# A projection chunk's matmul order: high weights on the front tokens first, then on the rear ones

## The reference

```python
x = x + 0.5 * swiglu(rmsnorm(x, p['ffn1_norm'][i]), p['ffn1_w_in'][i], p['ffn1_w_out'][i])
h = rmsnorm(x, p['mix_norm'][i])
...
x = x + y
x = x + cross_attend(rmsnorm(x, p['xattn_norm'][i]), mem_k[i], mem_v[i], p['xattn_w_q'][i], p['xattn_w_o'][i])
x = x + 0.5 * swiglu(rmsnorm(x, p['ffn2_norm'][i]), p['ffn2_w_in'][i], p['ffn2_w_out'][i])
```

```python
def swiglu(x, w_in, w_out):
    gate, up = jnp.split(x @ w_in, 2, axis=-1)
    return (jax.nn.silu(gate) * up) @ w_out
```

## Time and profile before

| | |
|---|---|
| runs | 2361.16, 2360.91, 2357.80 us; median 2360.91 |
| profiled execution, first to last instruction | 2357.9 us |
| PE busy | 2332.7 us (99%), 21043 matmuls |
| PEld busy | 2270.3 us (96%) |
| DVE busy | 1295.9 us (55%) |
| ACT busy | 869.0 us (37%) |
| POOL busy | 609.4 us (26%) |
| bytes moved | 289.19 MB, 123 GB/s over the span |
| the eight output halves begin at | 141, 344, 877, 1060, 1274, 1476, 2103, 2286 us |

### The profile page before, as it was taken

One profiled execution on the slowest core, in us unless ns is written; L12 is line 12 of the kernel. 1 busy time (PEld: TensorE's weight loads), 2 busy tenths in 40 slices (PEclk: granted clock), 3 DMA queues, 4 the chain that ended last, 5 costly groups with the idle time before them and its releaser, 6 DMA issues.

```text
span 2357.9 us, 50146 instructions
## 1 busy us (share of the span) xinstructions
PE 2332.7 (99%) x21043; PEld 2270.3 (96%) x21043; DVE 1295.9 (55%) x1906; ACT 869.0 (37%) x1399; POOL 609.4 (26%) x591
## 2 busy tenths in 40 slices
PE   8999999999999999999999999999999999999999
PEld 8999999889979999999999999999999979999999
DVE  6653643964576443445543344577777666443443
ACT  4422333453233321322433233267775233321323
POOL 4779967331103000004111010432122102000003
PEclk9999999999999999999999999999999999999999
DMA  6455445553562333333543333233332653333332
GB/s 167 128 161 149 123 134 169 171 170 107 166 242 84 98 99 91 96 96 99 158 117 111 100 108 115 83 100 108 104 111 77 213 188 91 97 94 94 98 94 94
DMA packets 483707, 289.19 MB, mean 123 GB/s; under 512 B 22289, under 2 KB 466962, under 8 KB 482514
## 3 DMA queue, kind: packets, MB, share of 16 engines
q1 hardware_dynamic: 477856, 280.66, 40.4%
q0 software_dynamic: 560, 1.84, 0.6%
q10 hardware_dynamic: 5122, 4.25, 0.5%
HBM read 258.86 MB, written 27.85 MB: 122 GB/s over the span
## 4 chain that ended last, share of the span: by engine, by line
PE 90%; DVE 4%; POOL 2%; ACT 1%; issue 1%; DMA 1%; SPq 0%; DVEq 0%; POOLq 0%; ACTq 0%
PE lin L3021 51%; PE lin L3026 25%; PE mis L2512 4%; POOL sTmp L737 1%; PE mis L2650 1%; PE lin L2600 1%; PE lin L2762 1%; PE mis L2633 1%; PE lin L2757 1%; PE lin L2983 1%; POOL sGe L738 0%; DVE w_lo L1827 0%; POOL sFe L738 0%; PE lin L2650 0%; PE mis L2626 0%
## 5 line engine op out<-in xcount | busy, mean ns | idle before, releaser
L1827 DVE TENSOR_TENSOR w_lo<-raw,w_hi 128x1024 fp32r<-128x1024 f32 (+1 forms) x322 | 464.0, 1441 | 294.4 <-ACT w_hi L1330 293.7
L1330 ACT ACTIVATE w_hi<-raw 128x1024 fp32r<-128x1024 f32 (+1 forms) x328 | 365.1, 1113 | 314.2 <-PE lin L3026 244.4
L3021 PE MATMUL lin<-a_rear,w_hi 128*128 128x264 f32 x3552 | 455.6, 279 | 0.0
L3021 PE MATMUL lin<-a_front,w_hi 128*128 128x256 f32 x3552 | 451.5, 279 | 1.1 <-DVE a_rear L1840 0.7
L3021 PEld LDWEIGHTS lin<-a_rear,w_hi 128*128 128x128 f32 x3552 | 432.6, 188 | 0.0
L3021 PEld LDWEIGHTS lin<-a_front,w_hi 128*128 128x128 f32 x3552 | 424.4, 188 | 4.5 <-issue 1.8
L3026 PE MATMUL lin<-a_rear,w_lo 128*128 128x264 f32 x1776 | 245.1, 278 | 0.0
L3026 PE MATMUL lin<-a_front,w_lo 128*128 128x256 f32 x1776 | 240.5, 277 | 1.0 <-DVE w_lo L1827 1.0
L2391 DVE SCALAR_TENSOR_TENSOR xT<-lin,xT 128x520 f32<-128x520 f32 (+1 forms) x87 | 60.9, 700 | 322.8 <-PE lin L3026 322.1
L1063 POOL TENSOR_TENSOR acc<-xT 128x520 f32<-128x520 f32 x8 | 12.2, 1521 | 864.6 <-DVE xT L2391 836.6
L3026 PEld LDWEIGHTS lin<-a_rear,w_lo 128*128 128x128 f32 x1776 | 223.8, 188 | 0.0
(11 more groups left out here) (512 smaller groups left out, 3181.5 us busy)
## 6 DMA issues: line engine op xcount, KB each, us to landing
raw<-in_ffn_w_in_dram SPq DMA_DIRECT2D x176, 512.0 KB, 3.9
raw<-in_ffn_w_out_dram SPq DMA_DIRECT2D x64, 704.0 KB, 4.6
kc<-in_cache_mem_k_dram SPq DMA_DIRECT2D x32, 512.0 KB, 7.1
vc<-in_cache_mem_v_dram SPq DMA_DIRECT2D x16, 1024.0 KB, 9.1
raw<-in_hg_w_in_dram SPq DMA_DIRECT2D x32, 512.0 KB, 4.3
raw<-in_xattn_w_kv_dram SPq DMA_DIRECT2D x16, 512.0 KB, 4.4
raw<-in_s_w_glu_dram SPq DMA_DIRECT2D x16, 512.0 KB, 4.0
raw<-in_xattn_w_q_dram SPq DMA_DIRECT2D x16, 512.0 KB, 3.9
```

What stands on the lines that cost most here:

```text
L1330: act.activation(w_hi[:, j, 0:kt, :], raw[:, j, 0:kt, :], ACT.Copy).then_inc(hi_ready, 1)
L1827: dve.tensor_tensor(low_weights(n, j), raw[:, j, 0:kt, :], w_hi[:, j, 0:kt, :].bitcast(F32), ALU.subtract).then_inc(lo_ready, 1)
L3021: pe.matmul(lpart(j, half), high[:, k, :], (x_lo if u else x_hi)[half][:, k, :], start=start and u == 0 and k == 0, stop=False)
```

## The change

In the plain chunks of the output halves the loop over the two token parts in the high-weight section is turned round. The low-weight section stays as it is, and so do first chunks and the last chunk of the program.

```diff
@@ -3056,7 +3056,7 @@
                         for half in range(2):
                             ins = low_weight_tiles(half, range(kt))
                     elif kt == FH:
-                        for half in (1, 0):
+                        for half in range(2):
                             for u in range(2):
                                 high_weights(half, u, range(kt), True)
                         pe.wait_ge(lo_ready, 2 * p + j + 1)
```

## The result

The changed kernel takes 2363.61 us in the median of 16 runs (2359.51 to 2366.14), the kernel before 2359.58 us in the median of 16 (2356.37 to 2365.20). The ratio is 1.0017 with a 95% interval of 1.0011 to 1.0024: 4.0 us slower by the medians, 2.6 to 5.7 us by the interval. That is clear of zero and just under the 0.2% that the prediction named as its bound.

A forecast was written before the change was run, and what follows sets the result against it. TensorE's matmuls were taken as the bound, covering 2332.7 of 2357.9 us. 50 chunks x 0.10 = 5.0 us plus 0.2 gave +5.2, so 2363.1, plus 3.0 from span to median: 2366.1 us (8 in 10: 2361.5 to 2370).

The forecast's parts named there:

- term 1: Front high as first group of a changed output-half chunk: 2.59 us instead of 2.49, so +0.10 us per chunk.
- the strict form: Moving rows: without a rear row followed by one at its own place modulo 256, all groups clean, a chunk of 7.60 us.
- Term 2: Rear high behind a slow front in changed chunks: today's 0.05 us excess is paid one group later, so zero.
- The seven second chunks: Chunks behind a half's first chunk: rear high would cost 2.62 us against 2.59 today, 7 x 0.03 = 0.2 us.
- The cover: First output half: five changed chunks ahead of 195.46 us lose 0.5 us, which disappears in TensorE's 2.85 us wait for POOL.
- the bound: Whole kernel: about 0.2%, 4.7 us, is what a measurement can tell from no change; the forecast lay just above it.
- A clean front entry: Rival at the changed chunks' entry: front high takes 2.49 us, 2.3 us less in all, 2358.6; chance 0.05.
- The slow pace: Rival: rear high doesn't recover behind a slow front in changed chunks, 8.5 to 14 us, 2369 to 2375; chance 0.07.
- The neutral case: Rival in changed chunks: front falls back to 113 ns on its own, total as much as today, 2360.9; chance 0.06.

The follow-up runs named there:

- the shift: The changed kernel with the rear tiles of f_* 128 bytes further on, order unchanged: 2359.5 us, the kernel before beside it 2361.4.
- the shift by 64: The changed kernel with the rear tiles of f_* 64 bytes further on: 2368.2 us against 2359.2 for the kernel before.
- the last kernel: The changed kernel with weight tiles at 0 modulo 256 and all f tiles 64 bytes further on: 2424.1 us against 2359.2 for the kernel before.
- the best kernel: The changed kernel with rear tiles 128 bytes on, low section rear first, first chunks' rear parts in turns: 2355.13 us, ratio 0.9985 to the kernel before.

## Why the prediction was right or wrong

**The direction and the mechanism of term 1** were right. Front high at an entry behind row 10 takes 2.59 us, the figure taken from the last chunk, in every plain chunk. The reason given, the place of rows modulo 256 and not the entry as such, was borne out by four kernels that moved the slow groups about by layout and order alone (the shift, rear first in the low section with it and without it, the kernel before with it). It was incomplete: it left out the weights, the strict form broke with the shift by 64, and it would make the second chunks slow, which they are not.

**Term 2, the rear group behind a slow front,** was forecast as no gain and no loss. It takes 2.606 us on the mean, 0.01 less than the 2.617 of the rear at the entry. So a plain chunk costs 0.087 us more and not 0.10.

**The seven second chunks** were sized wrong, in sign too. They were to cost 0.13 us each and they save 0.02 (7.598 us against 7.618 before). The prediction took a first chunk's end, where low rear runs as a pair at 125 ns, for an entry like the others. It isn't: behind it the front is back at 113 to 114 ns after two matmuls of 116. Why is open.

**The cover.** The five chunks ahead of the POOL wait were to lose 0.5 us, and the wait to shrink by as much. It is 2.85 us in both kernels. Of those five, one is a second chunk and two stand behind the small matmuls, where front first takes 7.71 us and rear first 7.73 to 7.76. Only two are plain, 0.09 us each. Nothing is there to be covered to speak of, and whether the wait would take it was not tested.

**The sum.** 42 plain chunks x 0.087 = 3.65; seven second chunks, -0.14; the chunk at 196 us behind small matmuls, -0.08 (behind the wait for POOL both profiles grant it the lower clock for a part, 0.66 on the mean from 195 to 200 us): +3.4 us, where the prediction had 5.2. The last chunk of the program, which the change leaves alone, adds 0.07 (see the rivals). Adding up the start-to-start times of all f matmuls from 300 us on gives 429.27 us before and 432.74 after, 3.5 us. The measured interval, 2.6 to 5.7 us, holds it. The error of 1.8 us is made up of the second chunks (1.1) and of 0.013 us per plain chunk (0.6, the part of term 1 and 2 that was mis-sized), with the chunk at 196 us for the rest. The time forecast, 2366.1, is 2.5 us above the 2363.6 measured; 1.3 us of this is the median of before, which came down from 2360.9 to 2359.6 with more runs; that the measured 4.0 us lie nearer to 5.2 than the groups' 3.5 do is luck, well within the interval.

**Against the bound.** 0.17% lies under 0.2%, so of the three outcomes it is "within 0.2%", which had 0.40 and not the highest chance. With the second chunks read rightly the forecast would have been under the bound.

**The rivals.** A clean front entry needs 2.49 us; it was 2.59. The slow pace doesn't last: low groups are 1.25 and 1.28 us, and the rear recovers after seven. The neutral case holds for the second chunks alone, where the front does fall back on its own. The evidence given for that case, the last chunk's low front of 1.27 us in the earlier trace rows, is particular to that place and doesn't always come there. In the changed kernel's run the same group, at the same entry and untouched by the change, takes 1.29 and stays slow, and the rear behind it takes 2.61 and not 2.57.

```profile
2339.96 2.75 PE L3084 MATMUL lin<-f_front,w_hi 128*128 128x256 f32 x22
2342.55 1.46 PE L3090 MATMUL lin<-f_front,w_lo 128*128 128x256 f32 x11
2343.85 2.77 PE L3084 MATMUL lin<-f_rear,w_hi 128*128 128x264 f32 x22
```

It isn't mere chance either. In three experiments the last chunk also enters slow at a good distance (rear first in the low section without the shift, the shift of 64, the last kernel), and in all three its low front falls back: 1.26, 1.27 and 1.25 us. What sets this place apart is that the low weights come late: before, VectorE's subtraction for this chunk runs from 2340.88 for 1.62 us, to 2342.50, and the low front starts at 2342.66; in the plain chunk of the earlier trace rows it ends 2.5 us ahead. The kernel with the shift and rear first in the low section was profiled twice: behind the same clean front its low front ends clean in one execution and stays slow in the other. So at this place the pace can change either way. That the late weights do it wasn't tested.

**Weight loads and moving rows.** The prediction put nothing for the place of the weights. With the same instructions in the same order, moving the weight tiles by 64 bytes took the program from 2363.6 to 2435.9 us, 3% more. "TensorE: Matmul & The Clock Gate" (section "Step-by-step: what each phase is for") says in the Trainium skill that loading the next tile's weights takes no SBUF read bandwidth from the running matmul. The runs here don't agree with that, since the place of the weights changes the matmuls' pace; what passes between the two isn't shown. The other rule that the prediction drew on, N/2.4 + 2.5 ns, stands in the Trainium skill, in the section "Back-to-back issue gap" of the same page, as the gap of an isolated matmul, so it was no rule for a stream of weight loads and matmuls. By it 256 columns would take 109.2 ns, an estimate; the clean pace here is 113.3.

## What to carry to other kernels

In a kernel bound by back-to-back matmuls, look at start-to-start times group by group: where a group of the same width costs 4% more than its like at the same granted clock, suspect the neighbour before it or places in SBUF; here neither busy shares nor waits showed it. Before reordering such a kernel, list for each kind of transition in the trace whether it is fast or slow, and count the new order's transitions from that list, each kind by its own row, the irregular ones too (here the second chunks). And let the order and the layout be chosen together: the same swap in the low section gained 0.09 us per chunk in one layout and lost 0.06 in the other.

## What was not expected of the hardware

- The distance of weight rows and moving rows in SBUF, modulo 256 bytes, sets the pace of fp32r matmuls: at 64 bytes from each other, 256 columns take 113.3 ns at best; at 0, 120 ns. For 264 columns it is 116.7 ns at best, and 122 where the distance is 0 and 128 in turn.
- At a good distance the pace still has two values, 113.3 and 118 ns for 256 columns, 116.7 and about 122 for 264. On rows that alternate the slow one ended in every case, within two to nine matmuls. On rows that keep one place it lasted to the end of the group in the plain chunks (22 of 22, and with low front ahead or behind 33 of 33), but ended within two matmuls in the second chunks of the changed kernel within three in the low front with the shift of 64 bytes, and within four in the low front of the last chunk of the kernel before.
- Behind a front group at the clean pace, a rear group that begins at 128 has two matmuls of 122 ns at its start (2.58 and not 2.57 us), which remains in the best kernel. Behind another rear group, in the low section of the same kernel, it has none.
